# Three special steps in every feed-forward pair, and joint low halves of a weight unit

## What is computed

```python
u = _rmsnorm(h, norm_mlp_g[layer])
a = jnp.einsum('bsd,df->bsf', u, w_up[layer])      # 2048 -> 8192
a = jnp.square(jax.nn.relu(a))
h = h + jnp.einsum('bsf,fd->bsd', a, w_down[layer])  # 8192 -> 2048
return _rmsnorm(h, norm_final_g)
```

## Time and profile before

| | |
|---|---|
| median of 3 runs | 2136.06 us (2136.01 to 2136.29) |
| the profiled execution | 2135.79 us |
| its span, first to last instruction | 2133.6 us |
| mean granted clock of PE | 0.999 of full speed |
| PE busy | 99% of the span |
| DVE busy | 62% |
| ACT busy | 49% |
| HBM | 188 GB/s over the span |

### The profile page before, as it was taken

The page is one execution under the profiler, slowest core; times in us unless marked ns, Lnnn a source line. Parts: engine busy times, 40 slices in busy tenths (PEclk is TensorE's granted clock), DMA queues, the critical chain, the costliest instruction groups (busy, mean ns, idle before and its releaser), DMA issues.

```text
span 2133.6 us, 25857 instructions
## 1 busy us (share of the span) xinstructions
PE 2111.0 (99%) x10130; PEld 1764.8 (83%) x10130; DVE 1317.1 (62%) x1675; ACT 1052.0 (49%) x1344; POOL 37.8 (2%) x49
## 2 busy tenths in 40 slices
PE   8999999999999999999999999999999999999998
PEld 7888888888888877788888888888888888888886
DVE  5874454555555776556554455456786787687675
ACT  6445454445444675454445444354544544454443
POOL 0000000000000020000000000000000000000000
PEclk9999999999999999999999999999999999999999
DMA  7455555564465544355755442455555455555453
GB/s 268 178 191 189 193 195 197 192 227 177 174 225 197 188 152 147 135 217 197 293 187 185 180 172 103 151 185 198 182 212 194 180 199 199 189 187 215 178 197 119
DMA packets 56550, 402.44 MB, mean 189 GB/s; under 512 B 6240, under 2 KB 6496, under 8 KB 9216
## 3 DMA queue, kind: packets, MB, share of 16 engines
q1 hardware_dynamic: 53648, 380.67, 49.5%
q0 software_dynamic: 2656, 19.81, 2.4%
q10 hardware_dynamic: 144, 0.52, 0.1%
HBM read 392.59 MB, written 8.39 MB: 188 GB/s over the span
## 4 chain that ended last, share of the span: by engine, by line
PE 97%; ACT 1%; issue 1%; DVE 0%; DMA 0%; SPq 0%; POOLq 0%; POOL 0%; DVEq 0%; ACTq 0%
PE proj L554 20%; PE proj L556 20%; PE proj L555 20%; PE proj L929 11%; PE proj L932 6%; PE proj L964 2%; PE proj L965 2%; PE tbank L530 2%; PE proj L963 2%; PE tbank L963 1%; PE tbank L964 1%; PE tbank L965 1%; PE bank_a L965 1%; PE bank_a L963 1%; PE bank_a L964 1%; PE bank_a L731 1%
## 5 line engine op out<-in xcount | busy, mean ns | idle before, releaser
L1554 DVE TENSOR_TENSOR w_lo<-raw,w_hi 128x1024 fp32r<-128x1024 f32 x714 | 861.5, 1214 | 717.8 <-ACT w_hi L1092 709.5
L1092 ACT ACTIVATE w_hi<-raw 128x1024 fp32r<-128x1024 f32 x714 | 748.5, 1052 | 958.7 <-PE proj L556 663.4
L554 PE MATMUL proj<-w_hi,a_both 128*128 128x512 f32 x1728 | 686.5, 397 | 0.0
L556 PE MATMUL proj<-w_hi,a_both 128*128 128x512 f32 x1728 | 674.1, 390 | 0.0
L555 PE MATMUL proj<-w_lo,a_both 128*128 128x512 f32 x1728 | 672.7, 389 | 0.0
L556 PEld LDWEIGHTS proj<-w_hi,a_both 128*128 128x128 f32 x1728 | 324.3, 188 | 69.2
L554 PEld LDWEIGHTS proj<-w_hi,a_both 128*128 128x128 f32 x1728 | 324.5, 188 | 68.5 <-issue 4.3
L555 PEld LDWEIGHTS proj<-w_lo,a_both 128*128 128x128 f32 x1728 | 324.8, 188 | 65.1
L929 PE MATMUL proj<-a_both,w_hi 128*128 128x512 f32 x1024 | 256.5, 392 | 0.3 <-DVE a_both L1597 0.3
L929 PEld LDWEIGHTS proj<-a_both,w_hi 128*128 128x128 f32 x1024 | 184.4, 189 | 33.7 <-DVE a_both L1597 0.5
L932 PEld LDWEIGHTS proj<-a_both,w_lo 128*128 128x128 f32 x1024 | 139.7, 190 | 10.0
(11 more groups left out here) (376 smaller groups left out, 1823.1 us busy)
## 6 DMA issues: line engine op xcount, KB each, us to landing
raw<-stream SPq DMA_DIRECT2D x359, 1024.0 KB, 4.8
nat<-x SPq DMA_DIRECT2D x4, 512.0 KB, 8.2
z_store<-z POOLq DMA_DIRECT2D x1, 2048.0 KB, 8.3
ga_store<-z POOLq DMA_DIRECT2D x1, 2048.0 KB, 12.5
gb_store<-z POOLq DMA_DIRECT2D x4, 512.0 KB, 7.1
yb<-z_store POOLq DMA_DIRECT2D x4, 512.0 KB, 6.8
ga<-ga_store POOLq DMA_DIRECT2D x1, 2048.0 KB, 8.2
gb<-gb_store POOLq DMA_DIRECT2D x1, 2048.0 KB, 14.5
```

The lines of the kernel that those rows point to most:

```text
L554: nc.tensor.matmul(banks[t][:, :], ah, wh, start=first, stop=False)
L556: last = nc.tensor.matmul(banks[t][:, :], al, wh, start=False, stop=end)
L1092: A((w_hi_end if extra else w_hi)[:, piece.n % RING, 0:width], src, ACT.Copy).then_inc(w_rounded, 1)
L1554: V.tensor_tensor(lo[:, s, 0:width], src, hi[:, s, 0:width].bitcast(f32), SUB).then_inc(w_rest, 1)
```

## The change

`SUM_AT` gets a third step, so steps 1, 3 and 4 (the second, fourth and fifth) of each of the seven pairs are special. In the feed-forward block DVE makes the low halves of a unit's two neighbouring pieces in one operation: at the first piece it only counts on, at the second it waits for both high halves (`w_rounded` for the second), subtracts over two places of the ring (2048 columns, or 1024 + 512 = 1536 for the raw pieces of a special unit) and counts `w_rest` up by two. `sum_weights(u + 1)` moves ahead of the low half of the first piece of unit u. Outside the feed-forward block each piece is handled as before.

```diff
--- before.py
+++ after.py
@@ -36,7 +36,7 @@
 UNITS = 1 + 4 * (4 + 4 + 8 + 4 + 2 + 8) + 14 + 4 * (4 + 4 + 4) + 4 * 8 + 4 * 4 + 4 * N_SLABS * 8
 
 STEPS = 8
-SUM_AT = (1, 4)
+SUM_AT = (1, 3, 4)
 PAIRS = 2 * N_SLABS - 1
 END_ORDER = (2, 3, 0, 1)
 UNITS_MLP = UNITS - N_SLABS * 32
@@ -1544,16 +1544,24 @@
                     if piece.reg is None and piece.n >= PIECES:
                         return
                     u, at, width, summed = WHERE[piece.n]
+                    if piece.reg is None and piece.n == FIRST_PIECE[u] and u + 1 in SUM_UNITS:
+                        sum_weights(u + 1)
                     s = piece.n % RING
-                    src = raw[:, u % RING, at:at + width]
-                    if summed:
-                        src = w_sum[:, SUM_UNITS.index(u) % 2, at:at + width]
-                    dve.wait_ge(w_rounded, piece.at(1))
                     extra = piece.reg is None and piece.n >= PIECES - RING
                     hi, lo = (w_hi_end, w_lo_end) if extra else (w_hi, w_lo)
-                    V.tensor_tensor(lo[:, s, 0:width], src, hi[:, s, 0:width].bitcast(f32), SUB).then_inc(w_rest, 1)
-                    if u + 1 in SUM_UNITS and piece.n == FIRST_PIECE[u]:
-                        sum_weights(u + 1)
+                    if piece.reg is None and u >= UNITS_MLP:
+                        if at == 0:
+                            piece.add()
+                            continue
+                        s = slice(s - 1, s + 1)
+                        dve.wait_ge(w_rounded, piece.at(1))
+                        src = w_sum[:, SUM_UNITS.index(u) % 2, 0:2 * PIECE] if summed else raw[:, u % RING, 0:at + width]
+                        flat = lambda buf: buf[:, s, :].rearrange("p a b -> p (a b)")[:, 0:at + width]
+                        V.tensor_tensor(flat(lo), src, flat(hi).bitcast(f32), SUB).then_inc(w_rest, 2)
+                    else:
+                        dve.wait_ge(w_rounded, piece.at(1))
+                        V.tensor_tensor(lo[:, s, 0:width], raw[:, u % RING, at:at + width], hi[:, s, 0:width].bitcast(f32),
+                                        SUB).then_inc(w_rest, 1)
                     piece.add()
 
             def sum_weights(u):
```

## The result

The changed kernel takes 2202.61 us (median of 4 runs, 2200.09 to 2203.86) against 2136.03 us (2135.67 to 2136.29): 1.031 times as long, 95% interval 1.0292 to 1.0328, or 66.6 us more. The forecast was 2193.1, with 2178 to 2208 around it. The direction and the mechanism hold; 9.5 us are not in the sum.

A forecast was written before the change was run, and what follows sets the result against it. TensorE was taken to bound the kernel, busy 2111.0 of 2133.6 us. Stalls in the pairs and edges, together 61.8 us, less 4.76 for removed matmuls, gave +57.0 on the median: 2193.1 us, range 2178 to 2208.

The forecast's parts named there:

- The removal: Step 3 becomes special in each of 7 pairs, so 24 matmuls become 21, all on PE's path: 4.76 us saved.
- The joint operation's length: DVE's joint low half of two pieces lasts 2.30 us at 2048 columns and 1.76 at 1536, by slope.
- rival A: The joint operation's release is hidden, PE loses nothing and the 21 matmuls are gone: 2131.3 us; chance 0.04.
- The main chain: Single pieces of the pairs followed through ACT, DVE and PE, giving PE stalls of 1.3 to 2.67 us.
- The wait at c: Third piece of special step 1: its joint low half needs the fourth piece's high half first, so PE stalls 1.80 us.
- h3 wait: Third piece of special step 4: PE stalls 1.80 us while the joint low half waits for the fourth piece's place.
- The sums ahead of e and f: Both pieces of step 2: DVE makes step 3's sum_weights first; PE stalls 2.67 us, or 2.07 in a pair after another.
- the passage: From one pair to the next: sum_weights delays the next pair's first joint low half; PE stalls 1.3 us, 3 times.
- The edges: Joint low halves delay PE by 1.07 us in the projection up's first chunk and 2.15 at the last projection.
- Rival D: PE's pauses in the pairs drop half of each pair's matmuls to 1.2 GHz: 137 us more, 2330; chance 0.02.
- The sign that the clock stays at 1.00: Expected in the changed kernel's trace: PE's granted clock remains at 1.00, its 2.4 GHz level, despite the new waits.

## Why the prediction was right, and where it fell short

**The removal.** 21 matmuls went, and the kernel with its sums spread gives back 4.9 us (2136.28 - 2131.42) where 4.76 were computed.

**The joint operation's length.** 2.29 measured at 2048 columns and 1.75 at 1536, against 2.30 and 1.76 from the slope of two shorter ones. The Trainium skill's rule in rival A (VectorE: DVE Perf Modes, The TRN2 errata: a fixed cost per instruction, paid once by a large tile) holds for these rows, 2.29 against two of 1.23, and the time still went the other way. Where the two short operations would stand right behind each other, the gain is smaller still: twice 1.14 against the 2.21 from 1527.19 to 1529.40.

**The main chain.** The wait at c was put at 1.80 and is 1.88. Nearly all of the missing 0.08 is the start of the joint operation: DVE began 0.10 us after the end of the high half (1526.03 + 1.06 to 1527.19), and 0.03 after it in the single ones. Why it is later I didn't test. Over the 21 waits of this kind 0.08 makes 1.7 us. The number of waits in the pairs, 31, was right, and no pair has one at a place that the chain didn't name. One h3 wait, in the sixth pair, is 1.84 idle in place of 1.57, in both traces of this kernel. The extra 0.27 comes in ahead of DVE: ACT starts the high half of h4 0.53 us after PE's next piece begins (1982.28 to 1982.81), and 0.26 after it in the fourth pair (1790.84 to 1791.10). Why ACT is late there stays unexplained.

**The sums ahead of e and f.** 2.67 and 2.07 forecast, 2.78 and 2.08 measured; the passage 1.3 and 1.46. Putting the sums behind took all three away, so it is the order and not the load. The first pair was to last 50.8 and the second 48.9; they last 52.77, of which 1.6 is the slow stretch, and 49.23.

**The edges.** 1.07 and 2.15 forecast. 1.14 (1.45 idle less 0.31 before) and 2.2 measured: the last 96 matmuls begin within 24.01 us in place of 21.77. The experiment with joint halves outside the pairs has both edges by themselves, and costs 3.4.

**The clock, the step that failed.** Rival D was dismissed with the sentence that "a pause of 1.8 to 2.7 should not lower it", on the strength of the first 20 us, where PE is idle for 8.35 us at a granted clock of 1.00. That is a misreading, for the clock was not at its upper level there. The trace of the kernel before has its first record of the granted clock at 18.2 us, and the column of the earlier trace rows counts time without a record as 1.00. The matmuls themselves show the level. Their timeline in that trace, all of 128x256:

```profile
17.65 0.41 PE L613 MATMUL proj<-a_both,w_hi 128*128 128x256 f32 x1
17.86 0.41 PE L614 MATMUL proj<-a_both,w_hi 128*128 128x256 f32 x1
...
18.36 0.28 PE L614 MATMUL proj<-a_both,w_hi 128*128 128x256 f32 x1
18.48 0.28 PE L615 MATMUL proj<-a_both,w_lo 128*128 128x256 f32 x1
```

They are 0.21 us apart up to 17.86 and 0.12 from 18.36 on, so PE ran at little more than half its pace before. Up to the rise it had worked without a gap since 12.26. The same trace has a fall after a short idle time as well. PE's last matmul ends at 2125.62, and 2.0 us later the granted clock is at half (table by stretch, columns as in the earlier trace rows):

```profile
2125.70:2127.60 1.90, 0.00 (x0) 0.00 (x0) 1.02 (x3) 0.72 (x2) 0.00 (x0) 1.00 0.00 0
2127.60:2133.60 6.00, 0.00 (x0) 0.00 (x0) 1.15 (x2) 1.15 (x1) 0.55 (x1) 0.50 0.47 175
```

The forecast's longest wait was 2.67, so the trace of the kernel before spoke against the dismissal, and not for it. The sign that the clock stays at 1.00 failed. In the changed kernel the clock fell four times, and with the waits filled it never did. The Trainium skill (TensorE: Matmul & The Clock Gate, Part 1) has an idle PE fall to half rate; the traces agree that it does. The size given to the rival, 137 us, was as wrong: a stretch costs 1.6, since it is short and the waits for DVE behind it aren't longer. A term for it belonged in the main case and not in a rival at 0.02; that the measured time still lies inside the forecast's range is owed to the width that the range had for other reasons.

Together: 31 waits in the pairs are 51.9 us idle and 9.6 for the 0.31 at each, 61.5; edges 3.4; clock 6.4; less 4.76. That is 66.5, and the medians differ by 66.6. (The span of the profiled execution grew by 67.0, of which 0.8 came ahead of the feed-forward block. Counted by the starts of the matmuls, the 31 waits are 60.8 and the sum 65.8, against 66.2 from the block on; so about 0.4 is open, and the agreement to 0.1 is in part luck.) Of the 9.5 us that the forecast lacked, the clock is 6.4. The other 3 are waits that are longer than forecast: 1.7 at c, g3 and h3, 0.5 each at e and at the passages, 0.3 at the one late h3, and 0.2 at the edges.

## What to carry to other kernels

An engine that makes things ready for another through a ring must be judged by when each piece is handed over, not by its busy share: joining two operations saves 0.16 us of its busy time and holds the first piece back until the second one's place is free, which costs nothing where the pieces between are long (2.7 us each) and 1.88 us where they are short. A chain by hand, with starts, durations and one rule for each semaphore, was right to 0.2 us at 30 of 31 waits, and the same chain shows where added work fits: three special steps gain 4.9 us when their sums stand in DVE's idle time, lose 4.2 where they stood by habit, and 66.6 with the sums ahead and the halves joined. Behind it, ask what waits of a microsecond or two do to PE's clock, and check a granted clock of 1.00 against the distance of the matmuls: early in these traces it stood for a time without a record.

## What the hardware showed that I had not expected

PE's granted clock fell to 1.2 GHz in a pair where PE was busy for 84% of the time (44.45 of 52.77 us) and never idle for more than 2.5 us at once; matmuls that add zero, put into its waits, kept it at 2.4 GHz and made the kernel 6.8 us faster. In the kernel before it fell 2.0 us after the last matmul. And two executions of one program with waits equal to 0.01 us had three and four such stretches.
